# The pre-norm vector of three FFN layers is multiplied onto the updated rows instead of onto the gate and up weights

## The reference

```
def rms_norm(x, g):
    y = xf * lax.rsqrt(jnp.mean(xf * xf, axis=-1, keepdims=True) + EPS)
    return (y * g.astype(jnp.float32)).astype(x.dtype)
def swiglu(x, w_gate, w_up, w_down):
    return (jax.nn.silu(x @ w_gate) * (x @ w_up)) @ w_down
def half_ffn(h, l, j):
    y = swiglu(rms_norm(h, ffn_norm_pre[l, j]), ffn_w_gate[l, j], ffn_w_up[l, j], ffn_w_down[l, j])
    return h + 0.5 * rms_norm(y, ffn_norm_post[l, j])
```

## Time and profile before

| | us |
|---|---|
| median of three runs | 2311.55 |
| lowest and highest run | 2310.42 and 2313.16 |
| span of the profiled execution | 2311.2 |
| PE busy in it | 2289.0 |
| DVE busy in it | 1336.2 |
| ACT busy in it | 977.3 |
| POOL busy in it | 73.6 |

### The profile page before, as it was taken

The page is one execution under the profiler, slowest core; times in us unless marked ns, Lnnn a source line. Parts: engine busy times, 40 slices in busy tenths (PEclk is TensorE's granted clock), DMA queues, the critical chain, the costliest instruction groups (busy, mean ns, idle before and its releaser), DMA issues. The chain is left out here.

```text
span 2311.2 us, 30089 instructions
## 1 busy us (share of the span) xinstructions
PE 2289.0 (99%) x11883; PEld 1940.0 (84%) x11883; DVE 1336.2 (58%) x1862; ACT 977.3 (42%) x1612; POOL 73.6 (3%) x115
## 2 busy tenths in 40 slices
PE   8999999999999999999999999999999999999998
PEld 7888888888888888888888888888878888888887
DVE  5857536596645646573355564346897574557334
ACT  5433324444444444443343433235266554444332
POOL 0000003000000000000010000000000000000000
PEclk9999999999999999999999999999999999999999
DMA  4332332311223223413323313333322222341321
GB/s 168 108 130 79 95 110 74 109 64 55 74 74 105 70 78 105 146 59 105 98 85 119 124 59 102 106 95 92 101 74 83 92 65 92 110 135 48 117 93 73
DMA packets 171650, 217.70 MB, mean 94 GB/s; under 512 B 13080, under 2 KB 123000, under 8 KB 171512
## 3 DMA queue, kind: packets, MB, share of 16 engines
q1 hardware_dynamic: 171400, 215.75, 29.0%
q10 hardware_dynamic: 112, 0.03, 0.0%
HBM read 213.63 MB, written 2.10 MB: 93 GB/s over the span
## 5 line engine op out<-in xcount | busy, mean ns | idle before, releaser
L2111 PE MATMUL ps<-xlo,whi 128*128 128x512 f32 (+1 forms) x2056 | 755.5, 367 | 2.1 <-DVE wlo L1324 2.1
L2112 PE MATMUL ps<-xhi,wlo 128*128 128x512 f32 (+1 forms) x2056 | 753.2, 366 | 0.0
L2113 PE MATMUL ps<-xhi,whi 128*128 128x512 f32 (+1 forms) x2056 | 753.0, 366 | 0.0
L1324 DVE SCALAR_TENSOR_TENSOR wlo<-raw,vec,whi 128x512 fp32r<-128x512 f32 (+1 forms) x488 | 340.8, 742 | 388.9 <-ACT whi L795 387.8
L795 ACT ACTIVATE whi<-raw,vec 128x512 fp32r<-128x512 f32 (+1 forms) x488 | 320.8, 709 | 445.4 <-PE ps L2113 390.5
L2111 PEld LDWEIGHTS ps<-xlo,whi 128*128 128x128 f32 x2056 | 388.6, 189 | 65.6 <-issue 2.7
L2113 PEld LDWEIGHTS ps<-xhi,whi 128*128 128x128 f32 x2056 | 388.4, 189 | 62.9
L2112 PEld LDWEIGHTS ps<-xhi,wlo 128*128 128x128 f32 x2056 | 388.6, 189 | 62.0
L1319 DVE TENSOR_TENSOR wlo<-raw,whi 128x1024 fp32r<-128x1024 f32 x104 | 126.7, 1223 | 183.1 <-ACT whi L791 182.3
L791 ACT ACTIVATE whi<-raw 128x1024 fp32r<-128x1024 f32 x104 | 109.5, 1057 | 199.7 <-PE ps L2113 199.3
L2111 PE MATMUL ps<-wlo,xhi 128*128 128x512 f32 x352 | 138.6, 394 | 1.0 <-issue 1.0
(11 more groups left out here) (291 smaller groups left out, 2909.5 us busy)
## 6 DMA issues: line engine op xcount, KB each, us to landing
raw<-ffn_w_gate_dram SPq DMA_DIRECT2D x176, 256.0 KB, 2.8
raw<-ffn_w_up_dram SPq DMA_DIRECT2D x176, 256.0 KB, 3.1
raw<-ffn_w_down_dram SPq DMA_DIRECT2D x96, 256.0 KB, 3.1
w<-ffn_w_down_dram SPq DMA_DIRECT2D x72, 256.0 KB, 5.3
raw<-xattn_w_kv_dram SPq DMA_DIRECT2D x64, 256.0 KB, 2.9
raw<-even_w_in_dram SPq DMA_DIRECT2D x56, 256.0 KB, 2.9
raw<-odd_w_in_dram SPq DMA_DIRECT2D x42, 256.0 KB, 2.9
raw<-xattn_w_q_dram SPq DMA_DIRECT2D x32, 256.0 KB, 3.0
```

Source lines behind the costliest of these rows:

```text
L1324: last = v.scalar_tensor_tensor(out=lo[:, k, :], in0=full[:, k, :], scalar=vec[:, c:c + 1], in1=hi[:, k, :].bitcast(f32), op0=MUL, op1=SUB)
L2111: mm(out_ap, lh, rl, start=start, stop=False, skip_group_check=skip_group_check)
L2112: mm(out_ap, ll, rh, start=False, stop=False, skip_group_check=skip_group_check)
L2113: return mm(out_ap, lh, rh, start=False, stop=stop, skip_group_check=skip_group_check)
```

## The change

The pieces of the gate and up weights lose their gains in the three scaled FFNs. SP loads the pre-norm vector, copied to all 128 partitions, into a new tile `pre_gain` behind the `post_gain` of the sublayer that ends there. DVE multiplies each updated tile of `h` by it into `y_rows` (`gain_rows`), right behind the update of that tile, after a wait for the update. ACT scales `y_rows` in place, and waits for `gain_rows` besides the power. `pre_gain` lies on the memory of `w11`, which is free at that time.

```
--- before.py
+++ after.py
@@ -206,6 +206,7 @@
     plain_lo = place("plain_lo", [P, 10, SEQ], f32r, at(MID))
     mid = place("mid", [P, 8, HALF], f32, at(2 * MID))
     w11 = place("w11", [P, 3, GC], f32, at(2 * MID + 2048))
+    pre_gain = place("pre_gain", [P, D], f32, at(2 * MID + 2048))
     w21 = place("w21", [P, 3, GC], f32, at(7 * NB + 1024))
     w12 = place("w12", [P, 3, GC], f32, ring_at)
 
@@ -289,6 +290,8 @@
     var_ready, rstd_ready, rstd_in_split, mean_ready, spread_ready, spread_used = map(sem, (
         "var_ready", "rstd_ready", "rstd_in_split", "mean_ready", "spread_ready", "spread_used"))
 
+    pre_gain_loaded, rows_gained = sem("pre_gain_loaded"), sem("rows_gained")
+
     gate_scaled, up_scaled, gate_silu, product_ready, sums_ready, mid_hi_ready, mid_lo_ready = map(sem, (
         "gate_scaled", "up_scaled", "gate_silu", "product_ready", "sums_ready", "mid_hi_ready", "mid_lo_ready"))
 
@@ -456,7 +459,7 @@
     for kind, l, arg, ng, n in STAGES:
         for g in range(ng):
             for i in range(group_pieces(kind, g, n, arg)):
-                gated = kind == "gate_up" or from_h(kind, arg)
+                gated = from_h(kind, arg) if kind != "gate_up" else not scaled_rows(kind, l, arg)
                 first = gain_of(kind, l, arg) if gated else None
                 wide = column_name(kind, g) == "c_f"
                 piece_gain.append(None if not gated else [first + k for k in range(KT)] if wide else
@@ -602,7 +605,7 @@
             return halves
 
         piece = ended = loads = 0
-        for kind, l, arg, ng, np_ in STAGES:
+        for n_stage, (kind, l, arg, ng, np_) in enumerate(STAGES):
             first_piece = piece
             if kind == "gate_up":
                 j, n = arg
@@ -661,6 +664,9 @@
                     sp.wait_ge(post_gain_used, ended)
                 sp.dma_start(post_gain[:], post_gain_rows(kind, l, arg).broadcast_to([P, D])).then_inc(post_gain_loaded, 16)
                 ended += 1
+                if opens_scaled(n_stage):
+                    _, l_next, (j_next, _), _, _ = STAGES[n_stage + 1]
+                    sp.dma_start(pre_gain[:], A["ffn_norm_pre"][l_next, j_next:j_next + 1].broadcast_to([P, D])).then_inc(pre_gain_loaded, 16)
         assert piece == total_pieces
 
         parts = [(t, 0, D) for t in range(TT - 1)] + [(TT - 1, 0, D // 2), (TT - 1, D // 2, D)]
@@ -876,7 +882,8 @@
 
             def scale_rows(t):
                 E.await_(input_rstd_ready)
-                E.run(a(y_rows[:, t, :], h[:, t, :], ACT.Copy, scale=rstd_in[:, t:t + 1]), rows_scaled)
+                E.await_(rows_gained)
+                E.run(a(y_rows[:, t, :], y_rows[:, t, :], ACT.Copy, scale=rstd_in[:, t:t + 1]), rows_scaled)
             if opens_scaled(n_stage):
                 square_tile(kind, second, 0, done + n)
                 next_h(0)
@@ -1506,6 +1513,13 @@
                     E.run(v.scalar_tensor_tensor(out=part, in0=y_rows[:, t, n_part * D // parts:(n_part + 1) * D // parts],
                                                  scalar=rstd[:, t:t + 1], in1=part, op0=MUL, op1=ADD), h_ready)
 
+            def gain_rows(t):
+
+                if t == 0:
+                    E.await_(pre_gain_loaded, 16)
+                dve.wait_ge(h_ready, E.made[h_ready.name])
+                E.run(v.tensor_tensor(y_rows[:, t, :], h[:, t, :], pre_gain[:], MUL), rows_gained)
+
             if kind == "down":
                 dve.wait_ge(pieces_used, done)
                 for t in range(TT):
@@ -1540,8 +1554,10 @@
                 E.run(v.tensor_scalar(var_in[:, t:t + 1], h_squares[:, t:t + 1], EPS, None, ADD), input_var_ready)
             if opens_scaled(n_stage):
                 update(0, take(0))
+                gain_rows(0)
                 row_variance(0)
                 update(1, take(1))
+                gain_rows(1)
                 split_next()
                 row_variance(1)
                 open_lo(0, x_banks[0])
@@ -1550,10 +1566,12 @@
                 made = take(2)
                 add_second(3)
                 update(2, made)
+                gain_rows(2)
                 made = weigh(3)
                 row_variance(2)
                 E.await_(input_rstd_ready, TT - 1)
                 update(3, made)
+                gain_rows(3)
                 split_next()
                 row_variance(3)
                 E.seen[input_rstd_ready.name] += 1
```

## The result

The changed kernel is slower by a little: its median is 2316.72 us (12 runs, 2315.5 to 2317.41) against 2311.51 us of the kernel before (12 runs, 2310.16 to 2313.17), a ratio of 1.002 with a 95% interval of 1.0012 to 1.0028. A second set of runs of the same two kernels gave 2316.43 against 2312.33 us, 1.002 (1.0011 to 1.0029). The profiled execution has a span of 2315.4 us, 4.2 us more than before.

The account below looks back on a forecast made before the run. PE was taken to bound the kernel, busy 2289.0 of 2311.2 us. The two `xo` places (1.46 us) and `down` (2.57) sum to 4.0 us, added to the median 2311.55: 2315.6 us, range 2313.3 to 2318.4.

Parts of the forecast that it names:

- three chains: Where a sublayer ends and a scaled FFN begins, near 835, 1200 and 1950 us; PE waits at each end; 4.0 us loss.
- `down` place: Into layer 1's first FFN near 1200 us, where PE already stands still: third piece 2.57 us later.
- `xo` places: Output projection into the second FFN of layers 0 and 1, near 835 and 1950 us: +0.73 us each, +1.46 together.
- The rival of a dearer handoff: Seven `gain_rows` handoffs in the chains; at 0.21 us each, 1.2 us more, so 2316.8 us; chance 0.25.
- The signs: Expected after: PE waits about 1.7 us for tile 1 and third piece at `down`, about 0.4 each at `xo`.
- the input variance of tile 2 at 847.91: Step at the first `xo` place: this variance on DVE starts at 847.91 instead of 847.27 us, 0.64 later.
- swallowed: At the `xo` places: tile 1's earlier shift, about +0.3 us, was taken as absorbed by the later one.
- Tile 3 finds its rows just in time: Behind the third piece at `down`: PE reaches tile 3's transposes with 0.14 us of cover; about as much at `xo`.
- The rival that the lock spills over: A held POOL power runs its full 0.93 us after DVE's end; tile 3's rows late, 1.2 us, 2316.8; chance 0.08.
- The loads and the shorter pieces at nothing: Three `pre_gain` loads hidden; shorter pieces count only in the chains. Rival, shorter pieces pay: 2310.2 us, chance 0.03.
- the forecast's own line of 4.6 us: Changes within 0.2% (4.6 us) were taken as about what a measurement can't tell from none; forecast 0.6 us inside.
- The clock falls: Rival at `down`: two close waits over 1 us lower PE's clock; 2.5 us lost, 2318.1 or more; chance 0.05.

Follow-up runs that it names:

- tile 1's order: Changed kernel with tile 1's input variance and the first open_lo ahead of the piece split on DVE: one run, 2313.95 us (before 2312.28).
- no-lock kernel: Changed kernel in which DVE waits for POOL's power of tile 3's input before the fourth piece: one run, 2315.12 us (before 2312.33).
- loads alone: Kernel before plus the three loads of `pre_gain`, which nothing reads: median 2311.89 us (before 2312.49), ratio 1.0.
- no gain: Changed kernel without the pre-norm vector of the three FFNs: plain pieces, no `gain_rows`, no load; median 2311.46 us (before 2312.49), ratio 0.9996.
- gain on top: Changed kernel whose pieces keep their gains beside `gain_rows` and its loads, so the vector is applied twice: median 2319.42 us (before 2312.49).
- changed again: The changed kernel unaltered, run and profiled once more beside new runs of the kernel before: median 2316.43 us (before 2312.33).
- tile 3's order: Changed kernel with only tile 3's `gain_rows` put behind the third piece and the input variance: one run, 2314.75 us (before 2312.28).
- two-gains kernel: Changed kernel with every `gain_rows` multiplication made twice, the second waiting for the first: one run, 2338.11 us (before 2312.33).

## Why the prediction was right, point by point

The forecast was a small real loss of 4.0 us in three chains. It was 4.25 us, in those places and no others. At `down` the steps hold one by one; at the `xo` places the near agreement is in part luck.

- *`gain_rows` and its handoff.* 1226 ns against 1.223 us; at `down` it starts 0.03 to 0.04 us after its update's end (1193.07 + 1.28 to 1194.38). The rival of a dearer handoff falls.
- *PE's waits before.* The 1.7 us "at one place" for a low weight part was misread as a wait for a piece that the change touches. In the timeline it is PE's first wait for a weight, at 12.80 us (1.74 us), for a piece that keeps its gains: the changed kernel has it too (1.75 us at 12.79). Only 1.0 of the 2.7 us thus stood where the change could win anything; the sum does not use them.
- *The `down` place.* 21.11 - 18.53 = 2.58 us against 2.57. Step by step it holds too: PE waits 1.76 us for tile 1 and 1.47 for the third piece where about 1.7 each stood in the forecast. The signs left out tile 2's rows, which the forecast's own +1.50 delays too: PE waits 0.76 us for them in place of 0.38, and so less for the third piece. The held power takes 0.92 us and the next starts at 1208.59, 0.37 us after the multiplication's end (1207.53 + 0.69).
- *The `xo` places.* 0.83 and 0.84 us against 0.73, in three errors that nearly cancel. The first is "the input variance of tile 2 at 847.91", which I let begin 0.08 us before the multiplication ended. In the rows it begins 0.14 us after that end:

```profile
844.45 1.29 DVE L1513 SCALAR_TENSOR_TENSOR h<-y_rows,rstd,h 128x1024 f32<-128x1024 f32 x1
845.77 1.23 DVE L1521 TENSOR_TENSOR y_rows<-h,pre_gain 128x1024 f32<-128x1024 f32 x1
846.91 0.15 DVE L1471 SCALAR_TENSOR_TENSOR var<-result_squares 128x1 f32<-128x1 f32 x1
846.98 0.69 DVE L1478 TENSOR_TENSOR y_rows<-ps,post_gain 128x512 f32<-128x512 f32 x1
847.81 0.15 DVE L1554 TENSOR_SCALAR var_in<-h_squares 128x1 f32<-128x1 f32 x1
```

  At an `xo` place the code behind tile 3's multiplication gives the banks free, and for that DVE waits for its own result; at `down` that wait isn't there and the variance does overlap (1208.13 against 1207.53 + 0.69). That is 0.22 us more. The wait as the cause is read from the code and the rows; no run took it away.

  The other two errors are in the start of tile 2's update, counted from tile 0's transposes: 9.58 us before (844.77 - 835.19), 9.45 after (844.45 - 835.00), 9.06 without the gain (844.11 - 835.05). So the shorter pieces, which I put at nothing here, bring it 0.52 us forward, and tile 1's shift, which I called "swallowed", puts it 0.39 us back: PE's last output products stand behind tile 1's transposes and come later with them. With tile 1's order alone the update starts at 9.06 us again (842.59 - 833.53), and the stretches get back 0.39 and 0.41 us; a shift that was swallowed would give back nothing.

```profile
842.59 1.28 DVE L1513 SCALAR_TENSOR_TENSOR h<-y_rows,rstd,h 128x1024 f32<-128x1024 f32 x1
```

  Together 0.22 - 0.52 + 0.39 = 0.09 us, which is what the forecast lacked. The two waits listed there, 0.2 and 0.3 us, were forecast at about 0.4 each.
- *Tile 3 finds its rows just in time.* So it was: the last power took 1.46 us and ended 0.40 us after the DVE instruction beside it (1212.98 + 1.46 against 1212.82 + 1.22), and PE reached tile 3's transposes without a wait, as in the no-lock kernel, whose rows came 0.9 us earlier. The rival that the lock spills over falls.
- *The loads and the shorter pieces at nothing.* The loads cost nothing (+0.02 us with the loads alone). The shorter pieces are worth nothing outside the places, but 0.86 us in them (no gain), of which the sum had only the parts at `down` and in the third piece. That matmul busy time flatters, as that rival says, shows in rows of the gain on top: products listed with 0.63 us each start 0.43 us apart.
- *The forecast of the median*, 2315.6 us, was 1.1 us low against the first set; the second set's difference of 4.1 us lies with the 4.0 of the sum. Against the forecast's own line of 4.6 us the first set's 5.2 us is over and the second set's 4.1 under; and both intervals leave out 1, so a measurement of this kernel could tell some 0.2% from none.
- *The clock falls*, with a chance of 0.05, was nearer than I gave it: at `down` the wait for tile 1 was 1.76 us at full clock, and 1.92 us in the gain-on-top kernel came before a fall.

## What to carry to other kernels

Where the bounding engine is 99% busy, 60 us of work saved on others were worth 0.86 us, and 14.7 us added cost 5.1 (from -0.86 to +4.25): look up what each edit does in the few places where that engine waits. Added work in a chain of handoffs costs by its place in the queue: behind the step that the next engine waits for, or beside another engine's part of the chain, the same twelve instructions cost 0.5 us. Where spans scatter by more than the effect, measure a stretch between two instructions of the bounding engine.

## What was not expected of the hardware

A wait only 0.16 us longer (1.92 against 1.76 us, each followed by eight transposes) went with a fall of PE's granted clock to 0.50 for some 3 us, which cost about 1 us there. The fall was seen in the one profiled run of the gain on top; four profiled runs with the wait of 1.76 us (changed, changed again, no lock, tile 3's order) kept 1.00. A chain made longer can so cost more than its length: in the two-gains kernel the stretches grew by 19.0 us where 15 were worked out without the clock. Where exactly the fall begins stays open, and no run varied the wait alone.

The scatter of the spans, in the two pairs of runs that I compared, lies in two stretches that the change does not touch, and PE's clock has a part in both. In the first 20 us of the profiled run of before, PE's first products behind the transposes took 0.41 us each at a granted clock listed as 1.00, in that of the loads alone 0.28 us; a product behind them starts at 575.8 and 573.6 us, and 2.2 us is what lies between the spans. In the changed kernel's second run products of 0.41 us stand where 0.50 is listed (first line), so a low clock that the list lacks is likely in the run of before too, but not shown. The other stretch is the low clock near 585 us: the two profiled runs of the changed kernel differ there (second and third line, first run and second).

```profile
14.00:16.00 2.00, 2.00 (x11) 2.00 (x11) 2.00 (x4) 2.00 (x4) 0.00 (x0) 0.50 1.02 389
580.00:600.00 20.00, 20.00 (x124) 17.00 (x123) 9.01 (x16) 6.76 (x18) 3.82 (x1) 0.74 0.16 53
580.00:600.00 20.00, 19.77 (x143) 16.31 (x143) 11.68 (x20) 8.79 (x22) 3.82 (x1) 0.91 0.25 81
```

A product ahead of it starts at 575.6 and 575.5 us, one behind it at 633.2 and 630.5: this is 2.6 of the 2.8 us between their spans. Why the same kernel gets one clock or the other is open.
